# A feed-forward layer's first weight sum loaded ahead of the input's combinations, and the last transposes one down product ahead

## What is computed

```python
D_FF = 2816
def swiglu(x, w_gate, w_up, w_down):
    return (jax.nn.silu(x @ w_gate) * (x @ w_up)) @ w_down

for i in range(2):
    ...
    u = rms_norm(h, ffn_norm_g[i])
    h = h + swiglu(u, ffn_w_gate[i], ffn_w_up[i], ffn_w_down[i])
```

## Time and profile before

| | |
|---|---|
| median of 3 runs | 1067.34 us |
| profiled execution | 1071.25 us |
| its span, first to last instruction | 1069.4 us |
| mean granted TensorE clock | 0.978 of full |
| TensorE matmul busy | 1010.9 us (95%) |
| VectorE busy | 722.3 us (68%) |
| ScalarE busy | 565.5 us (53%) |
| GpSimd busy | 156.4 us (15%) |
| moved by DMA | 210.55 MB, mean 197 GB/s |

### The profile page before, as it was taken

How to read it: one execution, slowest core, us unless ns; L and a number is a source line. 1 busy time by engine, 2 the same in 40 slices (tenths; PEclk the granted TensorE clock), 3 DMA queues, 4 the chain that set the end, 5 groups by cost and what they waited for, 6 DMA issues and landing times.

```text
span 1069.4 us, 13573 instructions
## 1 busy us (share of the span) xinstructions
PE 1010.9 (95%) x5422; PEld 854.5 (80%) x5422; DVE 722.3 (68%) x858; ACT 565.5 (53%) x685; POOL 156.4 (15%) x124
## 2 busy tenths in 40 slices
PE   9999929999989999992999998999999999999997
PEld 8977828888878888881888887888888888999886
DVE  6986638687857776763878775666554476777664
ACT  6326516566546777651655655665444543434533
POOL 4892510000010311161000001100000000000000
PEclk9999969999999999996999999999999999999999
DMA  8766877876644533457778654466555445455531
GB/s 317 227 203 114 289 198 232 279 252 228 228 151 163 187 130 119 172 202 206 245 259 274 233 199 158 158 226 236 180 195 197 157 163 191 176 187 191 197 118 40
DMA packets 33406, 210.55 MB, mean 197 GB/s; under 512 B 4024, under 2 KB 6584, under 8 KB 9280
## 3 DMA queue, kind: packets, MB, share of 16 engines
q1 hardware_dynamic: 24768, 173.55, 44.4%
q0 software_dynamic: 5552, 32.96, 12.1%
q10 hardware_dynamic: 3024, 3.18, 1.1%
HBM read 206.46 MB, written 3.21 MB: 196 GB/s over the span
## 4 chain that ended last, share of the span: by engine, by line
PE 84%; POOL 4%; DMA 4%; DVE 4%; ACT 2%; issue 2%; ACTq 0%; POOLq 0%; DVEq 0%
PE bank L395 56%; PE bank L517 11%; PE bank L381 4%; PE bank L383 4%; PE bank L382 4%; DMA arena<-in_ws 3%; PE bank L431 2%; DVE bank L2000 2%; POOL w_lo L1010 1%; POOL q_lo L1090 1%; PE bank L532 1%; DMA u_scr<-arena 1%; POOL arena L1087 1%; POOL arena L1086 1%; PE bank L622 1%
## 5 line engine op out<-in xcount | busy, mean ns | idle before, releaser
L1720 DVE TENSOR_TENSOR w_lo<-raw,w_hi 128x2048 fp32r<-128x2048 f32 x151 | 353.0, 2344 | 139.0 <-ACT w_hi L1177 138.5
L1177 ACT ACTIVATE w_hi<-raw 128x2048 fp32r<-128x2048 f32 x162 | 309.6, 1912 | 142.2 <-PE bank L395 112.7
L395 PE MATMUL bank<-w_hi,x_hi 128*128 128x512 f32 x608 | 167.1, 397 | 0.2
L395 PE MATMUL bank<-w_lo,x_hi 128*128 128x512 f32 x608 | 162.9, 390 | 0.0
L395 PE MATMUL bank<-w_hi,x_lo 128*128 128x512 f32 x608 | 162.9, 390 | 0.0
L395 PEld LDWEIGHTS bank<-w_hi,x_lo 128*128 128x128 f32 x608 | 114.1, 188 | 24.4
L395 PEld LDWEIGHTS bank<-w_lo,x_hi 128*128 128x128 f32 x608 | 114.1, 188 | 24.0
L395 PEld LDWEIGHTS bank<-w_hi,x_hi 128*128 128x128 f32 x608 | 110.6, 188 | 23.4 <-issue 1.8
L395 PE MATMUL bank<-w_hi,z_hi 128*128 128x512 f32 x320 | 94.3, 394 | 6.0 <-DVE z_lo L1814 5.9
L395 PE MATMUL bank<-w_hi,z_lo 128*128 128x512 f32 x320 | 92.8, 390 | 0.0
L395 PE MATMUL bank<-w_lo,z_hi 128*128 128x512 f32 x320 | 92.8, 390 | 0.0
(11 more groups left out here) (280 smaller groups left out, 1373.2 us busy)
## 6 DMA issues: line engine op xcount, KB each, us to landing
raw<-in_ws SPq DMA_DIRECT2D x162, 1024.0 KB, 4.9
arena<-in_ws POOLq DMA_DIRECT2D x24, 1024.0 KB, 10.0
arena<-u_scr ACTq DMA_DIRECT2D x16, 142.0 KB, 6.1
arena<-in_rows POOLq DMA_DIRECT2D x2, 1024.0 KB, 5.3
toep<-bias_row POOLq DMA_DIRECT2D x1, 1536.0 KB, 34.9
h<-in_x_tok SPq DMA_DIRECT2D x2, 512.0 KB, 4.0
raw<-in_ws SPq DMA_DIRECT2D x2, 512.0 KB, 7.8
arena<-in_rows POOLq DMA_DIRECT2D x2, 512.0 KB, 4.9
```

What stands on the lines that cost most here:

```text
L395: ins = pe.matmul(dst, tok(a_part, k, t), w_part[:, s, c], start=first and j == 0 and i == 0, stop=last and j == 2 and i == len(ks) - 1)
L1177: act.activation(w_hi[:, g % SPLIT, :], operand(g), ACT.Copy).then_inc(hi_done, 1)
L1720: dve.tensor_tensor(w_lo[:, g % SPLIT, :], operand(g), w_hi[:, g % SPLIT, :].bitcast(F32), ALU.subtract).then_inc(lo_done, 1)
```

## The change

The change has two parts. In the first, `q_f32` moves from slot 0 to slot 1 of the weight sums. The plain load of B11 for T1 of the first pair is issued on GpSimd's queue ahead of the combinations of the input. The accumulating load of B12 follows them, ahead of `q_lo`; it waits for the plain load. T4's two loads come after `q_lo` as before. VectorE's sum T2 of a layer's first pair gets a wait for `q_lo`, since it writes where `q_f32` lies. TensorE's wait for `q_lo` moves from the pair's begin to its second product. In the second part, the transposes behind a single step that has several down products come one product earlier. Only step 10 has several, so its order becomes: transposes of block 8, down product 9, transposes of block 10, down product 8, down product 10, where it was product 9, transposes 8, product 8, transposes 10, product 10. ScalarE's and VectorE's splits follow the same order.

```diff
-        q_f32 = view(5120, 4, 4, P)
+        q_f32 = view(7168, 4, 4, P)
...
# TensorE, single(i); the same in ScalarE (hidden_hi) and VectorE (hidden_lo), with ahead(...) for down(k)
-                    for j, k in enumerate(BEHIND.get(i, ())):
-                        if j:
-                            hidden_job(k)
+                    behind = BEHIND.get(i, ())
+                    for j, k in enumerate(behind):
+                        if j + 1 < len(behind):
+                            hidden_job(behind[j + 1])
                         down(k)
...
# TensorE, pair(p)
-                    if n == NPAIR * layer + 1:
-                        pe.wait_ge(S("q_lo"), layer + 1)
...
                     product(("p1", n), ffn_at(layer, p, "B11"), *of_x(0, t0), b1, True, (S("c_11"), 2 * n - 1))
                     hidden_job(turned[0])
+                    if n == NPAIR * layer + 1:
+                        pe.wait_ge(S("q_lo"), layer + 1)
                     product(("p5", n), ffn_at(layer, p, "T1"), *of_q(0), b4, True, (S("c_22"), 2 * n - 1))
...
# GpSimd
-            def input_sums(m):
-
-                layer = PAIRED.index(m)
+            def second_part(name, layer, p):
+
+                n = pair_no(layer, p)
+                if name == "T1":
+                    pool.wait_ge(S("t1_in"), 32 * n - 16)
+                    pool.dma_start(sums[:, 0, :], ws[B12_ROW[layer, p]], accum_op=ALU.add).then_inc(S("t1_in"), 16)
+                else:
+                    pool.wait_ge(S("t4_in"), 32 * n - 16)
+                    pool.dma_start(sums[:, 2, :], ws[PIECE_OF[ffn_at(layer, p, "B22")]], accum_op=ALU.add) \
+                        .then_inc(S("t4_in"), 16)
+
+            def first_sums(m):
+
+                layer, p = PAIRED.index(m), PAIRS[0]
+                pool.dma_start(sums[:, 0, :], ws[PIECE_OF[ffn_at(layer, p, "B11")]]).then_inc(S("t1_in"), 16)
                 for n_ in range(2):
                     for t in range(TT):
                         freed(pool, ("tr", m, n_, t))
...
                 pool.tensor_tensor(q_f32[:, 3, :, :], a11, a21, ALU.subtract).then_inc(S("q_sums"), 1)
+                second_part("T1", layer, p)
                 pool.wait_ge(S("q_hi"), layer + 1)
                 pool.wait_ge(S("q_sums"), layer + 1)
                 pool.tensor_tensor(flat4(q_lo), flat4(q_f32), flat4(q_hi).bitcast(F32), ALU.subtract).then_inc(S("q_lo"), 1)
+                for n_ in range(2):
+                    for t in range(TT):
+                        pool.wait_ge(*jobs[(m, n_, t)])
+                pool.dma_start(sums[:, 2, :], ws[B12_ROW[layer, p]]).then_inc(S("t4_in"), 16)
+                second_part("T4", layer, p)
...
# VectorE, second_sum(p)
                     if PAIRS.index(p):
                         lo_ready(dve, ffn_at(layer, PAIRS[PAIRS.index(p) - 1], "T3"))
+                    else:
+                        dve.wait_ge(S("q_lo"), layer + 1)
```

More of the change, by code:

```diff
@@ L1074, in h_factor, with flat4 @@
                 pool.tensor_tensor(st2[:, 2 * m:2 * m + 2], st2[:, 58:60], st2[:, 56:58], ALU.pow).then_inc(S("r_done"), 1)
-            def input_sums(m):
-                layer = PAIRED.index(m)
+            def flat4(z):
+                return z.rearrange("p i k c -> p (i k c)")
+            def second_part(name, layer, p):
[10 more added lines that the diff above has]
+                pool.dma_start(sums[:, 0, :], ws[PIECE_OF[ffn_at(layer, p, "B11")]]).then_inc(S("t1_in"), 16)
                 for n_ in range(2):
@@ L1090, in input_sums @@
                 pool.tensor_tensor(flat4(q_lo), flat4(q_f32), flat4(q_hi).bitcast(F32), ALU.subtract).then_inc(S("q_lo"), 1)
-            def flat4(z):
-                return z.rearrange("p i k c -> p (i k c)")
-            def weight_sums(layer):
[L1097 to L1104, removed]
-                    pool.dma_start(sums[:, 0, :], ws[PIECE_OF[ffn_at(layer, p, "B11")]]).then_inc(S("t1_in"), 16)
[L1106 to L1116, removed]
@@ new lines, in first_sums @@
+                for n_ in range(2):
[3 more added lines that the diff above has]
+                second_part("T4", layer, p)
+            def weight_sums(layer):
+                for before, p in zip(PAIRS, PAIRS[1:]):
+                    lo_ready(pool, ffn_at(layer, before, "T1"))
+                    sum_there(pool, layer, before, "T2")
+                    pool.dma_start(sums[:, 0, :], ws[PIECE_OF[ffn_at(layer, p, "B11")]]).then_inc(S("t1_in"), 16)
+                    lo_ready(pool, ffn_at(layer, before, "T4"))
+                    pool.dma_start(sums[:, 2, :], ws[B12_ROW[layer, p]]).then_inc(S("t4_in"), 16)
+                    second_part("T1", layer, p)
+                    second_part("T4", layer, p)
@@ L1118, in _ @@
             h_factor(0)
-            input_sums(0)
+            first_sums(0)
             weight_sums(0)
@@ L1137, in _ @@
             h_factor(3)
-            input_sums(3)
+            first_sums(3)
             weight_sums(1)
@@ L1265, in single @@
                                        ACT.Copy).then_inc(S("q_hi"), 1)
-                    for j, k in enumerate(BEHIND.get(i, ())):
-                        if j:
-                            hidden_hi(k)
+                    behind = BEHIND.get(i, ())
+                    for j, k in enumerate(behind):
+                        if j + 1 < len(behind):
+                            hidden_hi(behind[j + 1])
                         ahead(ffn_at(layer, "down", k))
@@ L1860, in single @@
                         second_sum(after)
-                    for j, k in enumerate(BEHIND.get(i, ())):
-                        if j:
-                            hidden_lo(k)
+                    behind = BEHIND.get(i, ())
+                    for j, k in enumerate(behind):
+                        if j + 1 < len(behind):
+                            hidden_lo(behind[j + 1])
                         ahead(ffn_at(layer, "down", k))
```

## The result

The changed kernel takes 1040.8 us (median of 4 runs, 1039.98 to 1042.93) against 1067.01 us for the kernel before (4 runs), a ratio of 0.9757, 95% interval 0.9737 to 0.9776: 26.2 us less. The forecast was 1039.1 us, range 1032 to 1050. The profiled execution of the changed kernel has a span of 1038.2 us and a mean granted clock of 0.988.

What follows compares the result with a forecast made beforehand. TensorE, busy 95%, loses time waiting for T1's arrival in both layers and on `z_lo` in step 10. Savings of 7.2 + 14.1 + 6.9 = 28.2 us against the 1067.34 us median give 1039.1 us, range 1032 to 1050.

Steps and rivals of the forecast that it cites:

- What bounds, and the chain from T1's arrival: TensorE's long wait before the pair's first product ends with T1's arrival in both layers; the product starts 4.8 us later.
- Layer 0: First feed-forward pair: B11 lands at 135.5, T1 at 144.5 against 151.66, 7.2 us earlier; ends 2.7 and 10.8.
- The price of an accumulating load: T1's accumulating load: 7.7 us alone, taken as 9.0 with a weight load beside it; bounds 7.7 and 10.5, far end 13.3.
- Layer 1: First pair: accumulating load issued right behind the combinations, T1 lands at 483.4 against 497.50, 14.1 us earlier; ends 9.8, 15.4.
- The Trainium skill's rule: DMA engines alternate between queues by packet, so B11 in layer 0 moves at half rate; without it 2.5 us better.
- The clock: First products in both layers: losses of 2.65 and 2.17 us to the halved clock are kept, nothing gained.
- Rival C: TensorE's clock stays up in layer 1, 2.2 us more gained; time 1036.9 us; chance 12%.
- Part 2: Step 10's transposes: 1.72 us saved each time, two times per layer, two layers, 6.9 us; ends 5.9 and 7.5.
- Rival A: Layer 0: B11 lands only around 141 because SyncE's loads and tables hold the engines; gain 0 to 2; 1045.3 us; 14%.
- Rival B: Layer 1: T4, loaded behind T1, is the next late, costing 1 to 3 us; about 1041.5 us; chance 12%.
- Rival D: GpSimd's wait for a slow B11 load delays T1, `q_lo` and T4 together; 1084.4 us at a 34.9 us load; 3%.
- Rival E: First product stays behind something other than T1, so only the step-10 transposes' change works; 1060.4 us; chance 3%.

Runs made afterwards that it cites:

- e5: Changed kernel with, in step 1, ScalarE's SiLUs before its cast of T1 and VectorE's gated products and sum T2 before T1's low part; 1030.33 us.
- e4: Changed kernel with SyncE's next weight loads, from B21's on, held in either layer until T1 has arrived; 1036.26 us.
- e6: Changed kernel with the bias tables' two loads issued after T4's loads on GpSimd's queue instead of ahead of B11's in layer 0; 1033.41 us.
- e3: Changed kernel with T1's accumulating load issued after `q_lo` instead of ahead of it; 1045.65 us.
- e2: Kernel before with only the second part of the change, the earlier transposes in step 10; 1059.81 us.
- e1: Changed kernel with step 10's transposes put back where they stood, so only the first part of the change; 1047.06 us.
- e7: Changed kernel with 55 (layer 0) and 24 (layer 1) extra 128 x 128 matmuls in TensorE's two long waits; 1038.83 us.
- e8: Changed kernel with SyncE held, tables and constants behind the sums, SiLU first, T1's accumulating load before the last combination, T4's first load before `q_lo`; 1022.72 us.

## Why the prediction was right, point by point

- **What bounds, and the chain from T1's arrival.** Right. From T1's landing to the first product there were 4.8 us before, and in the changed kernel 146.54 - 141.74 = 4.80 and 474.85 - 470.05 = 4.80. That the first product needs neither T1 nor `q` and hangs on the SiLU behind the cast was argued then; e5 shows it.
- **Layer 0: 7.2 us forecast, 6.0 measured.** The arrival of B11 was forecast 17.1 us after its issue and came after 16.4; the accumulating load was taken at 9.0 and took 10.75, beyond the 10.5 of the nearer bound, inside the 13.3 of the far one. B11's 0.7 us too few and the load's 1.75 too many offset each other in part, and that is luck. The mechanism given for B11's arrival was wrong in its last step, although the number was near: the sum lets all of B11 move after the tables have landed, for 5 us at half the rate beside SyncE's load. B11 did land 3.9 us after the tables (130.7 against 112.1 + 14.7), but e4 took SyncE's load away there and it landed 4.0 us after them, and GpSimd's queue moved only 0.3 MB in those last 4 us, so most of B11 had moved before. That the tables delay it was right: e6 moved them, and it came 7.4 us sooner.
- **The price of an accumulating load.** The working from traffic gave 7.7 us alone; e4 measured 8.04 and 8.0. The term that was mis-sized is the sharing: 1.3 us were put on it, where it was 2.7 in layer 0 (a weight load issued at the same moment) and 1.6 in layer 1. By that, one of the prediction's signs of being right, a load of less than 10.5 us, failed in layer 0; its sign of being wrong, more than 10.5 us even alone, didn't come.
- **Layer 1: 14.1 forecast, 13.6 measured.** GpSimd didn't wait for B11 there, which landed 8.4 us after its issue, and the load was issued right behind the combinations. e3 shows that its place ahead of `q_lo` carries 5.7 us of this.
- **The Trainium skill's rule** ("DMA: Bandwidth & Descriptors", "Queues, rings and completion order": an engine takes turns between queues packet by packet). e4's 10.75 to 8.04 us agrees that loads of two queues share the engines, and so do the 12 us of B11's flight in layer 0 in which the engines were full (114 to 126): GpSimd's queue moved 2.2 MB there and SyncE's 2.4. But the 2.5 us that the rule was made to give lay behind the tables' landing, and there e4 shows 0.2.
- **The clock.** Kept as lost, and mostly was: 0.7 us came back. Rival C (it stays up in layer 1) fell in the changed kernel, where the wait was 6.1 us and the clock went to 0.50 in it, and came true in e5, where it was 1.7.
- **Part 2: 6.9 forecast, 7.0 in the trace, 7.5 in e2 alone.** Transposes with a product behind them cost 292.14 - 291.78 = 0.36 us, as read from rows 9. From the transposes at the end of step 10's first half to the next layer stage's first matmul there were 317.98 - 290.27 us before and 304.10 - 279.90 now, 3.51 us less.
- **Rival A** (B11 lands around 141) fell: 130.7, which is 134.6 on the time scale of before. **Rival B** (T4 late): ScalarE cast T4 in layer 1 at 488.22, 13.4 us after the first product's start, behind an idle of 0.38 us that TensorE ended, as in rows 4. T4 had landed 6.4 us ahead of that (473.94 + 7.9), twice the margin given, since its accumulating load took 7.9 us and not 10.5. **Rival D** (a slow load holds T1, `q_lo` and T4 together) had its place right, since in layer 0 GpSimd did stand 6.15 us at the new wait with `q_lo` behind it, and its price wrong: nobody missed `q_lo`. **Rival E** fell with e1.
- **Sum.** 28.2 forecast, 26.2 measured: 1.2 us of it in layer 0, 0.5 in layer 1, the clock 0.7 the other way; the last 1.1 us is what the two profiled executions differ by more than the medians, beyond the 3.9 us of the front.

## What to carry to other kernels

Before a transfer is moved earlier in time, look at what stands in front of it in its own queue and at what runs beside it there: in layer 0 two loads ahead of the moved one cost it 7.4 us, and moving those gave as much as a quarter of the whole change, while as many bytes ahead of it in layer 1, with little beside, cost it 0.8 us. A wait can belong to an operand that the waiting instruction doesn't need, when the work that frees its bank stands in another engine's queue behind that operand's cast; swapping the two pieces of work, in ScalarE's queue and in VectorE's, gave 10.5 us, for no transfer made faster. And where a turn-round of 2.1 us stands between transposes and their product, another product between them hides all of it.

## What the runs showed of the hardware

- An accumulating load of 1 MB took 8.0 us from issue to landing with no load of another queue beside it (e4), where a plain one took 5.1 to 5.2 (before); traffic ran at 197 to 221 GB/s during accumulating loads and at 401 to 430 during plain ones (before). With a weight load beside it, it took up to 11.1 us (e7).
- In layer 0 a plain load of 1 MB behind the tables' 1.5 MB on the same queue landed after 16.4 us, and after 9.0 without them (e6). In layer 1 it landed after 8.4 us behind 1.5 MB of constants, and after 7.6 without them (e8). Taking away the load on another queue that lay beside the last 7 us in layer 0 changed the 16.4 by 0.2 us (e4).
- TensorE's granted clock fell to 0.50 in waits of 4.5 us (e4, layer 1), 6.1 us (changed kernel, layer 1) and longer, and stayed at 1.00 in those of 1.7 us (e5, layer 1) and 2.5 us (e8, layer 0). With small matmuls in the wait of layer 0 it stayed at 1.00 (e7).
- VectorE's low part of a weight piece took 2.29 us, and 5.0 us beside GpSimd's `q_lo`, ending 2.15 us after it; `q_lo` took 4.6 us with it.
